# Layer norm of the gated values dealt out behind the modulation groups, and another order of the weight pieces beside it

## The reference, cut to what matters

```python
mod = c_act @ w_mod + b_mod                  # 6 * 1024 columns, in the kernel 12 groups of 512
sh1, sc1, gt1, sh2, sc2, gt2 = split(mod, 6)
h = rms_norm(x, g_norm1) * (1.0 + sc1) + sh1
a_u, a_v, g_q, g_k, g_v, g_r, g_a, d_q, d_k, d_v, d_iq, d_ik, d_iw, gates = split(h @ w_in, cut)
v = layer_norm(gelu(a_v), ln_g, ln_b)        # the layer norm that the change moves
y_a = gelu(a_u) * (causal_mix(w_s, v) + b_s) # chunks of 128 tokens, four groups of 128 columns
# then gated linear attention, sparse attention, merging, a mixture of experts, a second block
```

## Time and profile before

| | us |
|---|---|
| median of 3 runs (1621.48 to 1624.85) | 1624.04 |
| the profiled execution | 1623.45 |
| its span in the profile | 1621.6 |
| TensorE busy | 1538.6 |
| VectorE busy | 962.6 |
| GpSimd busy | 886.2 |
| ScalarE busy | 553.6 |

### The profile page before, as it was taken

One profiled execution on the slowest core, in us unless ns is written; L12 is line 12 of the kernel. 1 busy time (PEld: TensorE's weight loads), 2 busy tenths in 40 slices (PEclk: granted clock), 3 DMA queues, 4 the chain that ended last, 5 costly groups with the idle time before them and its releaser, 6 DMA issues. The chain is left out here.

```text
span 1621.6 us, 20484 instructions
## 1 busy us (share of the span) xinstructions
PE 1538.6 (95%) x7541; PEld 1229.6 (76%) x7541; DVE 962.6 (59%) x1498; ACT 553.6 (34%) x1066; POOL 886.2 (55%) x827
## 2 busy tenths in 40 slices
PE   4999999999989998999998999999988999999998
PEld 2787888777768787787776886776766788888886
DVE  6695664779992648767765418766776532232235
ACT  3310433223352225667773124435446310010012
POOL 1756774647645726433346563242661676777674
PEclk9998999999999998999999999999999999999999
DMA  9446422422222107788775430111220223222221
GB/s 366 186 171 233 175 78 79 158 70 97 83 74 104 53 35 268 280 329 305 286 278 211 123 108 27 53 53 53 79 104 27 78 78 117 92 91 104 104 78 53
DMA packets 38823, 216.48 MB, mean 133 GB/s; under 512 B 5255, under 2 KB 10135, under 8 KB 15556
## 3 DMA queue, kind: packets, MB, share of 16 engines
q1 hardware_dynamic: 29352, 194.82, 32.8%
q10 hardware_dynamic: 7564, 14.56, 2.7%
q0 software_dynamic: 1808, 5.78, 1.0%
HBM read 207.20 MB, written 10.30 MB: 134 GB/s over the span
## 5 line engine op out<-in xcount | busy, mean ns | idle before, releaser
L2881 POOL TENSOR_TENSOR b_wlo<-b_raw,b_whi 128x512 fp32r<-128x512 f32 x441 | 610.0, 1388 | 203.9 <-ACT b_whi L1733 134.3
L2870 POOL TENSOR_SCALAR b_whi<-b_raw 128x512 fp32r<-128x512 f32 x364 | 266.2, 731 | 474.5 <-PE ps L542 420.9
L540 PE MATMUL ps<-b_hhi,b_whi 128*128 128x512 f32 (+1 forms) x984 | 392.1, 398 | 14.7 <-DVE b_hlo L1983 6.1
L541 PE MATMUL ps<-b_hlo,b_whi 128*128 128x512 f32 (+1 forms) x984 | 384.0, 390 | 0.0
L542 PE MATMUL ps<-b_hhi,b_wlo 128*128 128x512 f32 (+1 forms) x984 | 384.0, 390 | 0.0
L540 PEld LDWEIGHTS ps<-b_hhi,b_whi 128*128 128x128 f32 x984 | 186.3, 189 | 69.0 <-issue 23.5
L542 PEld LDWEIGHTS ps<-b_hhi,b_wlo 128*128 128x128 f32 x984 | 186.2, 189 | 39.5
L541 PEld LDWEIGHTS ps<-b_hlo,b_whi 128*128 128x128 f32 x984 | 186.4, 189 | 37.6 <-issue 1.2
L2518 DVE TENSOR_TENSOR b_wlo<-b_raw,b_whi 128x512 fp32r<-128x512 f32 x171 | 141.5, 870 | 64.0 <-ACT b_whi L1733 63.1
L1733 ACT ACTIVATE b_whi<-b_raw 128x512 fp32r<-128x512 f32 x240 | 142.3, 629 | 78.8 <-PE ps L542 46.7
L540 PE MATMUL ps<-b_whi,b_hhi 128*128 128x512 f32 (+1 forms) x368 | 144.4, 392 | 3.2 <-DVE b_hlo L1987 3.0
(11 more groups left out here) (410 smaller groups left out, 2149.9 us busy)
## 6 DMA issues: line engine op xcount, KB each, us to landing
b_raw<-in_stream SPq DMA_DIRECT2D x177, 1024.0 KB
bias_near<-bias_vectors ACTq DMA_DIRECT2D x1, 2298.0 KB
b_x<-in_xT SPq DMA_DIRECT2D x2, 1024.0 KB, 8.7
b_x<-in_xT ACTq DMA_DIRECT2D x1, 2048.0 KB, 8.2
h_tokens<-b_y SPq DMA_DIRECT2D x8, 256.0 KB, 2.3
b_arena<-in_cw ACTq DMA_DIRECT2D x1, 2048.0 KB, 10.9
out<-b_arena SPq DMA_DIRECT2D x8, 256.0 KB, 2.0
slot_outputs<-b_y ACTq DMA_DIRECT2D x3, 512.0 KB, 7.3
```

The source lines that it names most:

```text
L540: pe.matmul(o, ahi_, bhi_, start=start, stop=False)
L541: pe.matmul(o, ahi_, blo_, start=False, stop=False)
L2870: nc.gpsimd.tensor_scalar(whi[:, s, c], raw[:, r, c], 1.0, 1.0, ALU.mult, ALU.mult)\
L2881: nc.gpsimd.tensor_tensor(wlo[:, s, c], raw[:, r, c], whi[:, s, c].bitcast(F32), ALU.subtract)\
```

## The change

Two orders change; no instruction is added or removed. In `STREAM` each projection piece from `gqk0` to `gv1` moves ahead of the modulation pair that stood before it, so loads, VectorE's waits and raw buffers follow the new order. On VectorE the layer norm of chunk 0 stays where it was; chunk 1 goes behind `mod_sum(7)`, chunk 2 behind `mod_sum(9)`, chunk 3 between `mod_read(8)` and `mod_read(9)`, and the two router copies go behind `mod_read(9)`. The lists of TensorE, ScalarE and GpSimd stay as they were.

```diff
 STREAM = ([(f"mod{n}", 2) for n in range(4)]
-          + [("av", 2), ("au", 2), ("mod4", 2), ("gqk0", 1), ("mod5", 2), ("gqk1", 1), ("mod6", 2), ("misc0", 1),
-             ("mod7", 2), ("misc1", 1), ("mod8", 2), ("gv0", 1), ("mod9", 2), ("gv1", 1), ("merge0", 6), ("gr", 2),
+          + [("av", 2), ("au", 2), ("gqk0", 1), ("mod4", 2), ("gqk1", 1), ("mod5", 2), ("misc0", 1), ("mod6", 2),
+             ("misc1", 1), ("mod7", 2), ("gv0", 1), ("mod8", 2), ("gv1", 1), ("mod9", 2), ("merge0", 6), ("gr", 2),
@@
-            dve.wait_ge(sem("ln_rstd"), 1)
-            dve.wait_ge(sem("rows_in"), 16)
-            for c in range(ST):
+            def layer_normed(c):
                 v = gv_[:, c, :]
                 run(V.tensor_scalar(v, v, mv[:, c, 0:1], lnr[:, c:c + 1], ALU.subtract, ALU.mult))
                 run(V.tensor_tensor(v, v, rows[:, ROW["ln_g"]:ROW["ln_g"] + 512], ALU.mult))
                 run(V.tensor_tensor(v, v, rows[:, ROW["ln_b"]:ROW["ln_b"] + 512], ALU.add), "ln_done")
-            dve.wait_ge(sem("router_in"), 16)
-            run(V.tensor_copy(router[:, :, :], router_in))
-            run(V.tensor_copy(scol[:, 0:20], rows[:, ROW["b_router"]:ROW["b_router"] + 20]))
+
+            dve.wait_ge(sem("ln_rstd"), 1)
+            dve.wait_ge(sem("rows_in"), 16)
+            layer_normed(0)
             mod_read(4)
             mod_sum(6)
             mod_read(5)
             mod_sum(7)
+            layer_normed(1)
             mod_read(6)
             mod_sum(8)
             mod_read(7)
...
             mod_sum(9)
+            layer_normed(2)
             mod_read(8)
+            layer_normed(3)
             mod_read(9)
+            dve.wait_ge(sem("router_in"), 16)
+            run(V.tensor_copy(router[:, :, :], router_in))
+            run(V.tensor_copy(scol[:, 0:20], rows[:, ROW["b_router"]:ROW["b_router"] + 20]))
```

## The result

The changed kernel takes 1634.3 us (median of 5 runs, 1630.1 to 1637.9), the kernel before 1624.0; the ratio is 1.0065 (95% interval 1.0045 to 1.0085), so 7 to 14 us slower. The profiled execution took 1634.2 us.

A forecast was written before the change was run, and what follows sets the result against it. TensorE, busy 95% of the span, was taken as the bound. Terms 3.1 + 2.4 + 1.2 = 6.7 us on 1623.45 gave 1630.2, forecast as 1630.3 us, slower by 0.4%, range 1624 to 1634.5.

The forecast's parts named there:

- step 4: Ahead of the mix, TensorE waits for VectorE's layer norm chunk 3 behind product 8: +2.4 us, bounds +2.0 and +3.5.
- Step 1: Projection loads up to misc1: it starts at 118.8, TensorE's 3.7 us wait and clock fall go, 6.5 us gained meanwhile.
- the reserve of 1.5 us: At misc1: its first part is there at 120.8 to 121, TensorE wants it at 122.5.
- Step 2: Ahead of gv: VectorE must finish mod_sum(8) before reading product 7 and z, so gv starts at 147.0: +3.1 us.
- Step 3: In gv itself: the clock falls again at the same 2.4 us cost, no change, 1 us either way.
- by the same working: Behind the short products: 5.2 us at clock 0.50, costed as matmul time above the dense pace of 0.227 us, loses 2.4 us.
- the estimate worked out from that alone: Chunk 3 ahead of the mix: each of two products could wait out a GpSimd instruction of about 1.3 us, up to +4.3.
- step 5: Over the mix: TensorE's clock may fall behind the new wait; half a fall taken, +1.2 us, bounds 0 and +2.6.
- Step 6: Late statistics, chunks 1 and 2, router copies and VectorE 1 us later behind the mix: all hidden, costed at nothing.
- The reserve of 4.8 us at the first level product: Behind the mix: the next product needing VectorE starts at 206.30, its last input ready at 201.5.
- What comes behind the stretch moves along with it: Everything after the changed stretch depends on TensorE and shifts by the same amount, no further term.
- The third rival: misc1 lands late all the same, TensorE waits 2.5 us there, gv starts near 151: 1634.3 us; chance 0.09.

The follow-up runs named there:

- run 4: Changed kernel with mod_read(7) and the reads of z and iw moved ahead of mod_sum(8): 1624.2 us, ratio to before 1.0008.
- run 9: Changed kernel with gv alone in PSUM banks 1, 2, 6 and 7, all banks behind it as before: 1627.9 us, ratio to before 1.0025.
- run 6: Kernel before with the dealt layer norm alone (old STREAM), chunk 3 ahead of mod_read(8); measured twice: 1619.3 and 1618.1 us.
- Run 3: Changed kernel with layer norm chunk 3 moved ahead of mod_read(8): 1629.1 us, ratio to before 1.0042.
- run 1: Kernel before with the new STREAM order of pieces alone, VectorE's list as before: 1634.8 us, ratio to before 1.0073.
- run 5: Changed kernel with mod_read(7) and the z and iw reads ahead of mod_sum(8), and chunk 3 ahead of mod_read(8): 1623.7 us.
- run 8: Changed kernel with mod_read(7) and z, iw reads ahead of mod_sum(8), chunks 1, 2, 3 ahead of mod_sum(7), mod_sum(8), mod_sum(9): 1625.0 us.

## Why the prediction was wrong in size

Direction and mechanism came out as forecast, the size did not: 6.7 us were forecast, 10.7 measured between the two profiled executions (1623.45 and 1634.17 us), 10.3 between the medians. On these two traces the missing 4 us are 2.1 us inside the stretch, most of it in step 4, and 1.9 us behind it, where the forecast had none. By the prediction's own steps:

**Step 1, the chain of projection pieces: right.** `misc1` started at 120.11 (forecast 118.8), and TensorE did not wait for it. A step of the chain took 14.5 us, not 13.7, so the reserve of 1.5 us was nearly used up.

**Step 2, who needs the gain: right.** `mod_sum(8)` began at 137.2 (136.3 to 137.4) and ended at 146.3, `gv` began at 147.5 (147.0), in the second trace at 146.7. Runs 4 and 9 show from both sides that the banks of product 7 and `z` were the wait: VectorE's reads earlier, or other banks, and `gv` starts at 137. The step was forecast at +3.1 us and measured +3.6 against the same trace.

**Step 3, "the same 2.4 us: no change": right on its own trace (+0.1), but on an unsafe base.** The prediction has the 2.4 us "by the same working"; with its 14 matmuls that working gives 2.0, and against the 22.1 us that `gv` took in run 6 without fall or wait it is 2.2. More to the point, the fall of the clock behind `z` stood in the trace of before, and I took it for a property of the kernel. It isn't one: the second trace of before has none, and the two traces of run 6 have one each way. Over the ten traces in which `gv` follows the short products with no wait between, five have a fall there and five have none; in the three with 8.5 to 10.9 us of idle time ahead of `gv` (both of the changed kernel, and run 3) the clock is at 0.50 for 13.7 us each time, idle time included, from 139, 137 and 135 on (run 1, with 3.6 us of idle time there, has a fall too). So the change seems to make certain what otherwise comes by chance. Three traces and two of before don't prove it, and it is worth little: against the mean of its two traces before began `merge0` at 171.3, 2.2 us earlier than in the trace of the forecast, and only 1.0 of that lies behind `z`, the rest nearly all at `misc1`. Nor does it explain the miss of the median, since the forecast's trace was a typical execution in time (1623.45 us; of the five medians of before four are 1622.9 to 1624.0 and one is 1620.3): it was late in the stretch, and behind 300 us had as little time at the lower clock as any trace here. The prediction also has both falls come after about 4 us without dense matmuls; the second came 2.3 us into the short products, at 142.2.

**Step 4, the layer norm of chunk 3: the step that failed, in its size.** The start of the mix moved from 1.7 to 5.3 us behind product 8, +3.6 us in place of +2.4, in both traces (waits of 3.46 and 3.47 us). The term that was mis-sized is the chunk, taken at the mean of 2.75 us: it took 4.0. The mean was the wrong pick because the split of a `merge0` piece starts at the same time. Chunk 1, away from a split, took 2.0 us. All traces agree: each of the 16 chunks with GpSimd idle (to within 0.1 us) took 2.0 us, and each of the 29 with GpSimd at work for at least 2.8 us of it took 3.2 to 4.3, so the mean belonged to neither case, and the row of 3.8 us beside a split was the one to take. The Trainium skill's page "SBUF — State Buffer", section "Who interferes with whom", has an instruction of VectorE with two SBUF inputs blocked by GpSimd's; the estimate worked out from that alone gave up to +4.3, nearer than the mean. It came near partly by luck: it had both products wait 1.3 us, where the trace has them 0.3 and 0.9 us longer than in chunk 1, and the first instruction, which it left out, 0.8. Run 3 removes the chunk from that place and with it this wait and the fall of step 5.

**Step 5, the clock over the mix: +1.2 forecast, +1.4 measured** in the first trace, +2.7 in the second; half a fall was taken where one came each time. In sum, before rounding: 3.6 + 0.1 + 3.6 + 1.4 = 8.8 us (0.1 is `gv`, 24.4 us against 24.3).

**Step 6, costed at nothing: right for the changed kernel**, which has no other new wait of TensorE up to 300 us. The reserve of 4.8 us at the first level product is real, though, and is used up from the other side when TensorE comes early (runs 5 and 8).

**"What comes behind the stretch moves along with it": off by 1.9 us.** Up to 600 us it holds: the shift of 8.8 us at `merge0` is 8.4 there, and 8.4 in both places in the second trace. Behind that the first trace gained 1.9 us over the shift at `merge0`, the second 3.4. No instruction differs there. The time at the lower clock behind 300 us is 34 us in the forecast's trace, 38 in the second of before, 44 and 48 in those of the changed kernel, and 34 to 58 in all others. A microsecond of it costs at most a half, so the 10 us between the first two traces are enough for the 1.9. Fourteen traces don't settle whether it depends on a kernel at all, and this part stays open. So does why runs 5, 8 and 9 gave less in time than in the stretch, beyond the waits named.

**Luck.** The third rival, a late `misc1`, put its time at 1634.3 us, the median that was measured. That is chance: its wait for `misc1` did not occur, and `gv` began at 147.5, not near 151.

## What to carry to other kernels

Before loads are reordered or work is put into the gaps of an engine, look up which PSUM banks the engine ahead must get back, and from whom: here a read of 0.16 us stood behind 9 us of summing. Work dealt into a queue must not land between two steps that another engine is waiting for, least of all at the moment when GpSimd starts on work of its own. Such work is costed at the row that has the same neighbour, not at a mean over rows with and without one: here 4.0 us, not 2.75. And a fall of TensorE's clock in one trace is not a term of a sum until a second trace has it; behind 8.5 us or more of idle time all three traces had it.

## What the runs showed of the hardware

One and the same program came out with and without a fall of TensorE's clock at the same place (run 6: 1.00 over 22 us of `gv`, or 0.54 for its first 3.4 us). A VectorE chunk of three instructions took 2.0 us with GpSimd idle (16 of 16) and 3.2 to 4.3 us beside GpSimd's split (29 of 29), 4.0 in the changed kernel. Two series of the same kernel before differed by 0.2% in the median (1620.3 and 1623.5 us), with an interval of the ratio (0.9964 to 0.9998) that just left out 1.
